# The second feed-forward product of two layers by seven block products, with weight sums on GpSimd

## The reference

```python
def _layer(x, norm1, w_in, ..., w_out, norm2, w_ff1, w_ff2):
    ...
    x = x + jnp.concatenate([ya, yb, yc], axis=-1) @ w_out
    u = _rms(x, norm2) @ w_ff1
    return x + jnp.square(jax.nn.relu(u)) @ w_ff2

def first_block(x, ...):
    for l in range(DEPTH):
        x = _layer(x, norm1[l], w_in[l], ..., w_ff1[l], w_ff2[l])
    return x

def reference(x, ...):
    x = first_block(x, ...)
    x = second_block(x, ...)
    return x
```

## Time and profile before

| | |
|---|---|
| runs | 2924.66, 2921.14, 2916.51 us |
| median | 2921.14 us |
| span of the profiled execution | 2923.6 us, 45193 instructions |
| granted TensorE clock, mean | 0.969 of full |
| TensorE busy | 2783.6 us (95%) |
| VectorE, ScalarE, GpSimd busy | 1440.3, 988.4, 170.2 us (49%, 34%, 6%) |
| loads | 216.83 MB in all, mean 74 GB/s |

### The profile page before, as it was taken

One profiled execution on the slowest core, in us unless ns is written; L12 is line 12 of the kernel. 1 busy time (PEld: TensorE's weight loads), 2 busy tenths in 40 slices (PEclk: granted clock), 3 DMA queues, 4 the chain that ended last, 5 costly groups with the idle time before them and its releaser, 6 DMA issues.

```text
span 2923.6 us, 45193 instructions
## 1 busy us (share of the span) xinstructions
PE 2783.6 (95%) x20028; PEld 2299.7 (79%) x20028; DVE 1440.3 (49%) x2242; ACT 988.4 (34%) x1490; POOL 170.2 (6%) x166
## 2 busy tenths in 40 slices
PE   8989999999989999999999799999999897999998
PEld 7877888878768888887768778888887587788887
DVE  4575533344475444433454574343634645743436
ACT  4344322233344232323342233232333522332422
POOL 0200000001100000000013300000000033000000
PEclk9998999999989999999989899999999898999999
DMA  5102222223003222221000033222220001132221
GB/s 192 50 1 97 87 101 96 92 73 114 17 8 136 94 94 101 93 92 52 15 1 30 20 128 115 90 102 90 85 73 29 1 3 46 73 130 101 87 101 58
DMA packets 31011, 216.83 MB, mean 74 GB/s; under 512 B 3680, under 2 KB 3936, under 8 KB 6368
## 3 DMA queue, kind: packets, MB, share of 16 engines
q1 hardware_dynamic: 30816, 213.94, 20.2%
HBM read 211.83 MB, written 2.10 MB: 73 GB/s over the span
## 4 chain that ended last, share of the span: by engine, by line
PE 88%; DVE 8%; ACT 2%; issue 1%; PEld 0%; PEldq 0%; DMA 0%; ACTq 0%; SPq 0%; DVEq 0%
PE PS L570 81%; PE PS L573 3%; PE PS L771 2%; DVE SC L1381 2%; DVE X L1389 1%; DVE R L1381 1%; DVE SM L1392 1%; PE PS L1185 1%; PE PS L1135 1%; DVE LN L1381 0%; PE PS L855 0%; DVE SM L1381 0%; ACT LN L2172 0%; PE PS L764 0%; PEld PS L570 0%
## 5 line engine op out<-in xcount | busy, mean ns | idle before, releaser
L570 PE MATMUL PS<-H,SPL 128*128 128x512 f32 (+1 forms) x4560 | 1054.2, 391 | 5.5 <-DVE H L1389 4.0
L570 PEld LDWEIGHTS PS<-H,SPL 128*128 128x128 f32 (+1 forms) x4560 | 851.5, 188 | 188.5 <-issue 7.0
L1381 DVE TENSOR_TENSOR SPL<-RAW,SPL 128x2048 fp32r<-128x2048 f32 (+3 forms) x192 | 429.6, 2239 | 680.5 <-ACT SPL L2172 677.5
L2172 ACT ACTIVATE SPL<-RAW 128x2048 fp32r<-128x2048 f32 (+3 forms) x192 | 358.0, 1868 | 783.0 <-PE PS L570 754.8
L570 PE MATMUL PS<-SPL,Uu 128*128 128x512 f32 x2592 | 589.8, 389 | 0.0
L570 PEld LDWEIGHTS PS<-SPL,Uu 128*128 128x128 f32 x2592 | 486.5, 188 | 101.0
L570 PE MATMUL PS<-SPL,H 128*128 128x512 f32 (+2 forms) x2016 | 432.1, 375 | 2.3 <-DVE SPL L1381 1.6
L570 PEld LDWEIGHTS PS<-SPL,H 128*128 128x128 f32 x2016 | 363.7, 189 | 69.2 <-DVE SPL L1381 2.1
L2172 ACT ACTIVATE R<-PS 128x512 f32<-128x512 f32 (+1 forms) x154 | 88.5, 584 | 187.0 <-PE PS L570 156.3
L1381 DVE TENSOR_TENSOR R<-R,PS 128x512 f32<-128x512 f32 (+1 forms) x98 | 64.8, 661 | 106.6 <-PE PS L570 91.2
L2172 ACT ACTIVATE Uu<-R 128x512 fp32r<-128x512 f32 x108 | 68.3, 632 | 142.2 <-DVE R L1381 142.2
(11 more groups left out here) (240 smaller groups left out, 2481.7 us busy)
## 6 DMA issues: line engine op xcount, KB each, us to landing
RAW<-in_wA SPq DMA_DIRECT2D x84, 1024.0 KB, 4.8
RAW<-in_wB SPq DMA_DIRECT2D x84, 1024.0 KB, 4.8
RAW<-in_wAo SPq DMA_DIRECT2D x8, 1024.0 KB, 4.8
RAW<-in_wBo SPq DMA_DIRECT2D x8, 1024.0 KB, 5.0
LN<-in_ln SPq DMA_DIRECT2D x4, 1024.0 KB, 6.6
P<-in_pB SPq DMA_DIRECT2D x2, 1920.0 KB, 9.1
...
```

The lines of the kernel that those rows point to most:

```text
L570: return pe.matmul(out, l_, r_, start=start, stop=stop)
L1381: return v.tensor_tensor(out, a, b, o)
L2172: return a.activation(out, in_, f, scale=scale)
```

## The change

In every pass of layers 0 and 1 the second product, a matrix of 512 tokens x 1024 by one of 1024 x 1024, is seen as 2 x 2 blocks: A in blocks of 256 tokens x 512, B (weights) in blocks of 512 x 512. Seven products of such blocks, Strassen's scheme in Winograd's form, replace eight. A block product is 24 matmuls of 128 x 512 (two token tiles, four blocks of rows, three parts).

- Right factors, in the order of use: B11, B21, T2, T4, T3, T1, B22 with T3 = B22 - B12, T2 = B11 + T3, T4 = T2 - B21, T1 = B22 - T2. GpSimd forms the four sums in place in the raw buffers (`weight_sum`), and each factor is split as a weight group was. The order of the loads and the buffers of each pass come from `load_plan`; the four blocks of a pass must lie in raw buffers at once, so there are four: `RAW` twice, the new `RW2` and `LN`.
- Left factors: A11, A12, S2, A22, S3, S1, S4 with S3 = A11 - A21 (VectorE, `difference`), S2 = A22 - S3, S1 = A21 + A22, S4 = A12 - S2 (GpSimd, in place). Each is split to `Uu` by ScalarE (`high_operand`) and VectorE (`low_operand`); A12 in two halves.
- The activation: the token's root is now multiplied in ahead of the square. TensorE spreads the roots over the partitions once a layer (`spread_roots`), ScalarE copies them to RB. VectorE takes max(u, 0) x RB out of PSUM into `R` or the new `RU2`, ScalarE squares it there.
- The products P1, P2, P6, P4, P7, P5, P3 use banks 0-1, 2-3, 0-1, 4-5, 0-1, 6-7, 6-7. P6, P7 and P3 are added in PSUM to what their banks hold, and wait until VectorE has read it (`s.xadd`). VectorE adds banks to X (or subtracts them) 16 times a pass, before 8.
- `square` writes elsewhere, semaphores are renamed, the space for DMA descriptors is made smaller to make room.

The pieces of the diff, in order: tables, load plan, operands, TensorE, VectorE (difference, second product, pass), ScalarE (pass, second product), GpSimd, SyncE.

```diff
+QUADS = ((0, 1, 2, 3), (0, 1, 2, 3), (), ())
+PRODUCTS = ("P1", "P2", "P6", "P4", "P7", "P5", "P3")
+FACTORS = ("B11", "B21", "T2", "T4", "T3", "T1", "B22")
+HELD = {"B11": "B11", "B21": "B21", "T2": "B11", "T4": "B21", "T3": "B12", "T1": "B11", "B22": "B22"}
+SUMS = {"T3": 1, "T2": 2, "T4": 3, "T1": 4}
...
+                held = dict(zip(("B21", "B12", "B11", "B22") if p else ("B11", "B12", "B22", "B21"), ring))
+                landed = {}
+                for name, slot in held.items():
+                    landed[name] = load(l, at + BLOCKS[name], slot)[1]
+                quads.append((l, p, len(splits), held, landed, sums))
+                for name in FACTORS:
+                    if name in SUMS:
+                        split(held[HELD[name]], None, sums + SUMS[name])
+                    else:
+                        split(held[name], landed[name])
+                sums += 4
+                ring = [held[n] for n in ("B21", "B12", "B11", "B22")]
...
+        RU = [R[:, 10240:12288].rearrange("p (k s) -> p k s", k=4), RU2[:, 0:2048].rearrange("p (k s) -> p k s", k=4)]
...
+        EARLY, LATE = slice(0, 256), slice(256, 512)
...
+        A21, A11, A22, A12 = (RU[k][:, :, ts_] for k in range(2) for ts_ in (EARLY, LATE))
+        S3, S2, S1, S4 = A11, A11, A21, A12
+        RB = SM[:, 0:512]
...
+        OPERANDS = {"A11": (0, A11), "S3": (1, S3), "A12": (2, A12), "S2": (3, S2), "A22": (4, A22), "S1": (0, S1),
+                    "S4": (2, S4)}
+        LEFT = {"P1": ("A11", 1), "P2": ("A12", 3), "P6": ("S2", 4), "P4": ("A22", 5), "P7": ("S3", 2), "P5": ("S1", 6),
+                "P3": ("S4", 7)}
+        PBANKS = {"P1": (0, 1), "P2": (2, 3), "P6": (0, 1), "P4": (4, 5), "P7": (0, 1), "P5": (6, 7), "P3": (6, 7)}
...
+            def spread_roots(l):
+                pe.wait_ge(s.nr, 8 * (l + 1))
+                bank_free(4)
+                for t in range(4):
+                    ins = mm(bank(4)[:, t * 128:(t + 1) * 128], rms[t][:, 1:2].to_broadcast([128, 128]), C("ident"))
...
+                    which, lows = LEFT[name]
+                    ah, al = operand(OPERANDS[which][0])
+                    pe.wait_ge(s.lo, i + 1)
+                    pe.wait_ge(s.ul, ready + lows)
+                    goes_on = (name, 0) in added_to
+                    for b in range(2):
+                        if goes_on:
+                            pe.wait_ge(s.xadd, base + added_to[name, b])
+                        else:
...
+                            pe.matmul(out, ah[:, sl], wh, start=k == 0 and not goes_on, stop=False,
+                                      skip_group_check=True)
+                            pe.matmul(out, ah[:, sl], wl, start=False, stop=False, skip_group_check=True)
+                            ins = pe.matmul(out, al[:, sl], wh, start=False, stop=k == 3, skip_group_check=True)
+                        assert done_mm(ins) == full_at[(*key, name), b]
...
+                tt(S3, A11, A21, ALU.subtract).then_inc(s.us, 1)
+                v.wait_ge(s.us, n("us"))
...
+                low_parts()
+                low_operand("A12", slice(2, 4))
+                add("P1", 0, 2, 0, True)
+                add("P1", 1, 3, 0, True)
+                low_operand("S2")
+                low_parts()
+                add("P2", 0, 2, 0)
+                add("P2", 1, 3, 0)
+                low_operand("A22")
+                low_parts()
+                add("P6", 0, 2, 1, True)
...
+                add("P7", 0, 0, 0)
+                add("P7", 0, 0, 1, True)
+                add("P7", 1, 1, 0)
+                add("P7", 1, 1, 1, True)
+                add("P5", 0, 0, 1)
+                ended(0)
+                low_parts()
+                add("P5", 1, 1, 1)
+                ended(1)
+                low_parts()
...
+                    def squared(q, b):
+                        v.wait_ge(s.mm, full_at[(l, "up", p, q), b])
+                        stt(RU[q][:, b], bank(sets[q][b]), 0.0, RB, ALU.max, ALU.mult).then_inc(s.fv, 1)
+                    paid()
+                    low_parts()
+                    low_parts()
+                    v.wait_ge(s.rc, l + 1)
+                    for b in range(4):
+                        squared(0, b)
+                    low_parts()
+                    low_operand("A11")
+                    difference()
+                    low_parts()
+                    low_operand("S3")
+                    for b in range(3):
+                        squared(1, b)
+                    low_operand("A12", slice(0, 2))
...
+                    for b in range(4):
+                        squared(0, b)
+                    a.wait_ge(s.fg, n["fg"])
+                    high_operand("A11")
+                    high_parts()
+                    a.wait_ge(s.us, n("us"))
+                    high_operand("S3")
+                    high_parts()
+                    squared(1, 0)
+                    squared(1, 1)
+                    a.wait_ge(s.fg, n["fg"])
+                    high_operand("A12", slice(0, 2))
+                    squared(1, 2)
+                    squared(1, 3)
+                    a.wait_ge(s.fg, n["fg"])
+                    left = quad((l, "down", p), "rms" if p == 3 and l == 0 else None)
...
+                high_operand("A12", slice(2, 4))
+                high_parts()
+                a.wait_ge(s.gs, n("gs"))
+                high_operand("S2")
+                high_parts()
...
+                a.wait_ge(s.mm, full_at[(*key, "P1"), 1])
+                a.wait_ge(s.gs, n("gs"))
+                high_operand("S1")
+                high_parts()
+                a.wait_ge(s.mm, full_at[(*key, "P2"), 1])
+                a.wait_ge(s.gs, n("gs"))
+                high_operand("S4")
+                high_parts()
...
+                g.wait_ge(s.raw[held["B12"]], landed["B12"])
+                g.wait_ge(s.raw[held["B22"]], landed["B22"])
+                weight_sum("T3", B["B12"], B["B22"], B["B12"], ALU.subtract)
+                g.wait_ge(s.lo, j + 1)
+                g.wait_ge(s.tw, sums + 1)
+                weight_sum("T2", B["B11"], B["B11"], B["B12"], ALU.add)
+                g.wait_ge(s.lo, j + 2)
+                g.wait_ge(s.tw, sums + 2)
+                weight_sum("T4", B["B21"], B["B11"], B["B21"], ALU.subtract)
+                g.wait_ge(s.uh, highs + 4)
+                g.wait_ge(s.ul, lows + 2)
+                tt(S2, A22, S3, ALU.subtract).then_inc(s.gs, 1)
+                n("gs")
+                g.wait_ge(s.lo, j + 3)
+                g.wait_ge(s.tw, sums + 3)
+                weight_sum("T1", B["B11"], B["B22"], B["B11"], ALU.subtract)
+                tt(S1, A21, A22, ALU.add).then_inc(s.gs, 1)
+                n("gs")
+                g.wait_ge(s.ul, lows + 3)
+                g.wait_ge(s.gs, n["gs"] - 1)
+                tt(S4, A12, S2, ALU.subtract).then_inc(s.gs, 1)
+                n("gs")
+                n("ul", 7)
+                n("uh", 8)
...
+                if freed is not None:
+                    sp.wait_ge(s.lo, freed)
+                sp.dma_start(raw_slots[where][:, 0:w], src).then_inc(s.raw[where], 16)
...
-    nc = _bacc.Bacc("TRN2", target_bir_lowering=False, num_devices=1)
+    nc = _bacc.Bacc("TRN2", target_bir_lowering=False, num_devices=1, dynamic_dma_scratch_size=1024)
```

More of the change, by code:

```diff
@@ L1440, in chunk, with paid, low_operand @@
                             evict(b)
+            def paid():
+                while at["owed"]:
+                    at["owed"] -= 1
+                    low_parts()
+            def low_operand(which, ks=slice(0, 4)):
+                i, a_ = OPERANDS[which]
+                hi, lo = operand(i)
+                v.wait_ge(s.uh, n("uh"))
+                ins = tt(four(lo)[:, ks], a_[:, ks], four(hi)[:, ks].bitcast(f32), ALU.subtract)
+                if ks.stop == 4:
+                    ins.then_inc(s.ul, 1)
+                    n("ul")
@@ L2894, in gpsimd @@
                 fence()
+                for p in QUADS[l]:
+                    quad(l, p)
             for l in range(2):
@@ L2910, in sync @@
             sp.dma_start(PSM[:, 0:NPS], ap["psm"]).then_inc(s.psm, 16)
-            for i, (src, w) in enumerate(stream):
+            for i, (l_, k_, where, landed, freed) in enumerate(loads):
+                src, w = stream[first_load(l_) + k_]
                 if i == 3:
```

364 lines of the change are left out of this document (294 added, 70 removed).

## The result

| | before | after |
|---|---|---|
| median of the runs on one chip | 2922.48 us (8 runs) | 2940.15 us (8 runs) |
| range | 2916.51 to 2933.09 | 2935.91 to 2945.55 |
| ratio, 95% interval | | 1.0058, 1.0043 to 1.0073 |
| span of the profiled execution | 2923.6 us | 2941.6 us |

The change makes the kernel slower by 0.6%, some 17 us. The forecast was 2909 us; what came is rival (a), which was given 2946 us.

The account below looks back on a forecast made before the run. TensorE's gapless matmul stream was taken as the bound. Eight passes at 84.6 instead of 87.04 us (-19.5), spread_roots +2.2 and clock +5 gave -12.3 off median 2921.1: 2909 us; own range 2899 to 2919, whole range 2893 to 2948.

Parts of the forecast that it names:

- rival (a): GpSimd gets its turn between two VectorE operations, T2's sum before S3; pass 89.9 us, 2946 us; chance 0.32.
- What bounds the kernel: TensorE's stream: 88% of the chain, the changed stage one gapless run of matmuls, 87.04 us a pass.
- the matmuls removed: Second product of each pass: 168 matmuls instead of 192, 5.44 us less a pass, 43.5 us in eight.
- The sizes of the operations: Operations beside TensorE: weight sum 4.67 us on GpSimd, rest of a factor 2.30 on VectorE, eviction 0.75.
- No load was late: SyncE's weight loads, reordered into four buffers, were costed at nothing.
- The walk without collisions: A pass with VectorE and GpSimd not holding each other up: TensorE stands 1.8 us at P2, pass 83.4 us.
- rival (b): VectorE and GpSimd collisions cost nothing, falling into VectorE's spare time: pass 83.4 us, 2894 us; chance 0.08.
- VectorE keeps its turn: Shared port: VectorE runs A11's rest and S3 through before waiting GpSimd's T2 sum; P2 stands 2.5 us, pass 84.6.
- over 5 us: Sign for rival (a): S3 stretched to over 5 us and P2 standing over 5 us.
- 2.5 us at P4: In rival (a), P4 is 2.5 us late, part of 8.3 us of standing in a pass.
- The clock: Half clock behind P2's gap: 1.7 us in every second pass, less 2 us, 5 us in all.
- the forecast's own case: VectorE keeps its turn: standing 3.0 us a pass, mostly at P2, pass 84.6 us, 2909 us; chance 0.48.

Follow-up runs that it names:

- e8: Kernel after the change, T2's sum behind S3, A12's second rest ahead of T2's, T1's sum behind S2's rest, all seven GpSimd operations on few columns: 2888.0 us.
- e2: Kernel after the change with all seven GpSimd operations of a pass cut to a few columns (four weight sums, differences S2, S1, S4): 2901.9 us.
- e5: Kernel after the change with A11's rest and S3 on VectorE written as back-to-back pieces: 2946.2 us with 256 columns, 2964.4 us with 64.
- e6: Kernel after the change with each weight sum on GpSimd formed as two back-to-back halves of 128x1024: 2920.4 us.
- e3: Kernel after the change with one more wait on GpSimd, T2's sum waiting until VectorE has finished S3: 2930.0 us.
- e1: Kernel after the change with the four weight sums of each pass on 2 of their 2048 columns: 2916.8 us.

## Why the prediction was wrong

**What bounds the kernel, and the matmuls removed:** right. 81.6 us are what e8 has, 24 x 0.2267 less a pass. spread_roots took 1.05 us a layer with no wait of its own, 2.1 in all where 2.2 was said; in the timeline of the kernel after:

```profile
307.69 1.05 PE L699 MATMUL PS<-CST,SM 128*128 128x128 f32 x8
```

**The sizes of the operations:** right. T3's sum, alone, takes 4.62 us (4.67 said from the earlier trace rows); an eviction 0.69 (0.75 said from the earlier trace rows). The page of the Trainium skill that the prediction set beside it, "GPSIMD Engine Reference" (3.1), has 4497 ns on GpSimd and 2293 ns on VectorE; the runs show 4.62 and 2.29 us. With its two figures side by side the way out was there to be read: half the time on the shared port. No load was late: T3's sum starts 8 us before T2's is released.

**The walk without collisions:** right in the pass. It gave a standing of 1.8 us and a pass of 83.4; e2 has 1.45 and 83.3. That case was rival (b), 2894 us; e2 has 2902, four runs from 2891 to 2905.

**The step that failed** is this one: "I take it that VectorE keeps its turn through a run without gaps." Here it does not. S3 followed A11's rest at once and still waited for the whole sum, 5.62 us for 1.22; e5 shows it behind the first of 32 pieces, e6 the other way round, e3 that it is worth 10 us. Rival (a) had the place right: the sum between A11's rest and S3, a standing of 5.6 us at P2 (4.8 measured; its own sign was "over 5 us"), pass 89.9 (89.1), 2946 us (2940). That its total came so near is in part luck: it had no term for the clock, about 2.4 us a pass, and it had 2.5 us at P4 that did not come.

Rival (a) was kept at 0.32 because of one row, the GpSimd operation of 1.31 us in the earlier trace rows. The operations just before it, in the trace of the kernel before, show how it was held:

```profile
1482.18 0.76 POOL L2744 TENSOR_TENSOR HA<-HA,CST 128x64 f32<-128x64 f32 x1
...
1482.07 0.69 DVE L1381 TENSOR_TENSOR SC<-SC 8x512 f32<-8x512 f32 x1
1482.79 0.69 DVE L1389 SCALAR_TENSOR_TENSOR SM<-SC,SM 8x512 f32<-8x512 f32 x1
```

The one at 1482.18 ends at 1482.94, 0.18 us behind the VectorE operation that it met (1482.76). The one at 1482.90 met VectorE's at 1482.79, which ends at 1483.48; it ended at 1484.21, 0.19 us behind the four pieces (1484.02). So its times do fit a wait through all four, and 0.55 us of its 1.31 have no other explanation here. e5, with VectorE pieces of the same 64 columns, a sum of 2048 columns on GpSimd and 0.13 us from piece to piece, shows no such wait. So "VectorE keeps its turn" may hold for that row, and it fails at the place that decides this kernel; what makes the difference is open. The step took its rule from one row, with a GpSimd operation of 64 columns, against the others that had slipped in.

The rule of the Trainium skill's page "SBUF — State Buffer" (Who interferes with whom), that the one that starts first has the shared port for the whole instruction, spoke for rival (a). The runs agree with it: whatever waited got the port only when the holder's instruction had ended.

**The clock** was mis-sized too. It was put at 5 us in all, 3.4 us at half clock in every second pass. At a standing of 4.8 us it is 6.8 us at half clock in each of eight, about 2.4 us a pass, 19 us. P2's standing of 1.45 us (e2) has none of it in any pass; 1.95 us (e1) has it in seven of eight passes, 1.6 us each; behind the 2.04 us of e3 it comes in five. So the forecast's own case would probably have been dearer as well. e3 has nearly its standing, 3.1 us a pass where the forecast had 3.0, though split otherwise between P2 and P4, and its passes take 86.3 us, not 84.6; it came to 2930 us, not 2909. By this, an estimate, the kernel would have been about as fast as before even with the turns as I took them.

**P4**, late by 2.5 us in rival (a)'s walk, is not late in the trace. The last thing that it needs is A22's rest:

```profile
451.79 2.23 DVE L1555 TENSOR_TENSOR Uu<-RU,Uu 128x1024 fp32r<-128x1024 f32 x1
...
454.18 0.42 PE L919 MATMUL PS<-SPL,Uu 128*128 128x512 f32 x1
```

The rest ends at 454.02, and P4 starts at 454.18 with no wait. P2 started at 440.86; two products at full clock (48 x 0.2267 us) would have brought P4 to 451.7, and it would have stood 2.3 us, an estimate. So the half clock behind P2 and the wait at P4 take each other's place. That is why the pass came out as 89.1 us, and not as 89.9 with the clock on top; e3's two passes show the same exchange.
